# Gated linear attention prepared in 512-token parts beside the input projection, then run over 128-token pairs

## Time and profile before

| | us |
|---|---|
| median of 3 runs (2667.71 to 2677.51) | 2677.27 |
| profiled execution, its own time | 2677.31 |
| its span, first to last instruction | 2675.6 |

### The profile page before, as it was taken

The page is one execution under the profiler, slowest core; times in us unless marked ns, Lnnn a source line. Parts: engine busy times, 40 slices in busy tenths (PEclk is TensorE's granted clock), DMA queues, the critical chain, the costliest instruction groups (busy, mean ns, idle before and its releaser), DMA issues. The chain is left out here.

```text
span 2675.6 us, 34555 instructions
## 1 busy us (share of the span) xinstructions
PE 2281.3 (85%) x13572; PEld 1952.5 (73%) x13572; DVE 1440.0 (54%) x2273; ACT 954.2 (36%) x1399; POOL 360.6 (13%) x331
## 2 busy tenths in 40 slices
PE   7889999999247546629994799999999999999994
PEld 2368888888036346418883699999999999999993
DVE  3610016760576775276667555556555555555557
ACT  3611111111344232372220144444444444444444
POOL 1101000001320120020001101111111111111120
PEclk9899999999555565659996799999999999999997
DMA  7521101221222200534336256666656666665564
GB/s 268 190 59 68 65 24 64 73 102 47 63 54 72 62 8 17 212 128 164 115 114 231 94 204 221 220 220 220 212 203 202 215 218 202 208 215 203 204 215 192
DMA packets 161502, 392.50 MB, mean 147 GB/s; under 512 B 11988, under 2 KB 39412, under 8 KB 157332
## 3 DMA queue, kind: packets, MB, share of 16 engines
q1 hardware_dynamic: 136676, 299.89, 32.1%
q0 software_dynamic: 23600, 83.24, 9.9%
q10 hardware_dynamic: 1152, 8.39, 0.8%
HBM read 323.13 MB, written 68.35 MB: 146 GB/s over the span
## 5 line engine op out<-in xcount | busy, mean ns | idle before, releaser
L55 PE MATMUL bh<-xt_hi,shi 128*128 128x256 f32 x2048 | 580.5, 283 | 3.0 <-DVE slo L1859 3.0
L56 PE MATMUL bh<-xt_lo,shi 128*128 128x256 f32 x2048 | 580.4, 283 | 0.0
L57 PE MATMUL bh<-xt_hi,slo 128*128 128x256 f32 x2048 | 580.4, 283 | 0.0
L1859 DVE TENSOR_TENSOR slo<-raw,shi 128x1024 fp32r<-128x1024 f32 x384 | 455.6, 1222 | 155.4 <-ACT shi L1799 150.9
L1799 ACT ACTIVATE shi<-raw 128x1024 fp32r<-128x1024 f32 x384 | 388.9, 1050 | 130.6 <-PE eby L57 130.6
L55 PEld LDWEIGHTS bh<-xt_hi,shi 128*128 128x128 f32 x2048 | 394.1, 192 | 3.9 <-issue 3.4
L56 PEld LDWEIGHTS bh<-xt_lo,shi 128*128 128x128 f32 x2048 | 394.0, 192 | 0.6
L57 PEld LDWEIGHTS bh<-xt_hi,slo 128*128 128x128 f32 x2048 | 394.0, 192 | 0.0
L55 PE MATMUL bank<-h_hi,whi 128*128 128x512 f32 (+1 forms) x736 | 287.4, 391 | 7.3 <-DVE wlo L452 7.3
L56 PE MATMUL bank<-h_lo,whi 128*128 128x512 f32 (+1 forms) x736 | 287.2, 390 | 0.0
L57 PE MATMUL bank<-h_hi,wlo 128*128 128x512 f32 (+1 forms) x736 | 287.2, 390 | 0.0
(11 more groups left out here) (315 smaller groups left out, 3605.0 us busy)
## 6 DMA issues: line engine op xcount, KB each, us to landing
raw<-in_exp_w_dram SPq DMA_DIRECT2D x96, 2048.0 KB, 12.4
adaw<-in_ada_w_dram POOLq DMA_DIRECT2D x20, 1024.0 KB, 7.3
uT<-stage POOLq DMA_DIRECT2D x72, 256.0 KB, 2.3
wraw<-in_w_in_dram SPq DMA_DIRECT2D x22, 512.0 KB, 3.8
xb<-in_x_dram SPq DMA_DIRECT2D x16, 512.0 KB, 6.9
xt<-in_x_dram SPq DMA_DIRECT2D x16, 512.0 KB, 4.2
x2d<-xt SPq DMA_DIRECT2D x16, 512.0 KB, 2.6
h2d<-h SPq DMA_DIRECT2D x16, 512.0 KB, 2.9
```

The lines of the kernel that those rows point to most:

```text
L55: nc.tensor.matmul(out, w_hi, x_hi, start=start, stop=False)
L56: nc.tensor.matmul(out, w_hi, x_lo, start=False, stop=False)
L57: return nc.tensor.matmul(out, w_lo, x_hi, start=False, stop=stop)
L1859: nc.vector.tensor_tensor(item_dst(slo, n), item_src(n), item_dst(shi, n), ALU.subtract).then_inc(S["w_lo_ready"], 1)
```

## The change

It has three parts.

1. **Projection.** The tiles are in another order (decay inputs, keys, queries and values first, the gate last). TensorE's work is a list of slots, one unit each, in four banks; stage buffers are three, `wraw` is one. From slot 21 on, every third slot begins one of 20 parts: a head's 256 context tokens or 512 of its latent tokens. A part's work is dealt over the slots: logits and value transposes in its first (TensorE), Abs, Exp, Ln (ACT), scans (DVE); factors (ACT), keys (DVE), queries (POOL) in its second; transposes of the decayed keys ahead of the third slot's unit and four state updates (one per 128-token pair) behind it. The parts' inputs are loaded from `uT` by SP. Results go to DRAM: per head six arrays `prep` of 128 x 2048 (1 MB each), the transposed values, and `upd`, 18 pair updates. The decay bias is a 33rd row of the logits' product. The convolution works in two halves of 128 channels, its value taken from PSUM by DVE; the first half's taps are dealt over slots 52 to 74, the second's over slots 84 to 98.
2. **Heads.** The stage loads what was prepared. The state steps run over 128-token pairs: 16 in each direction and head, heads 0 and 1 first and interleaved, those of heads 2 and 3 behind the first four masks. The masks keep the whole 128 x 128 block, and two products of 64 x 64 per pair give the part of it between the two chunks. A state product has 128 columns.
3. **Last norm.** The squares of rows 0 to 7 move ahead in the last expert, the rows are scaled between the splits in smaller portions, and all groups but the first get their roots from ACT as Ln and Exp.

Core of the diff (lines that begin with # say where):

```diff
@@ phase_project @@
-    tiles = ([(OFF_A, "b")] + [(OFF_K + P * i, "b") for i in range(6)]
-             + [(256, "g"), (384, "g"), (0, "a"), (128, "a")]
-             + [(OFF_Q + P * i, "u") for i in range(2)] + [(OFF_R + P * i, "r") for i in range(4)]
-             + [(OFF_SC + P * i, "u") for i in range(6)])
+    V_OF = [OFF_V + P * h for h in range(HEADS)]
+    tiles = ([(OFF_A, "b"), (OFF_K, "b"), (OFF_Q, "u"), (V_OF[0], "b"), (V_OF[1], "b"), (OFF_K + P, "b"),
+              (OFF_Q + P, "u"), (V_OF[2], "b"), (V_OF[3], "b"), (256, "g"), (0, "a")]
+             + [(OFF_SC + P * i, "u") for i in range(6)] + [(384, "g"), (128, "a")]
+             + [(OFF_R + P * i, "r") for i in range(4)])
+    units = [(i, n) for i, (_, kind) in enumerate(tiles) for n in range(5 if kind == "b" else 4)]
+    NS = 3
+    START, PERIOD = 21, 3
+    parts = [(h, p) for h in range(HEADS) for p in range(5)]
+    begins = {START + PERIOD * j: j for j in range(NJ)}
+    NSLOT = max(NU + 1, START + PERIOD * NJ + 2)
 # SP, in its order per slot u: weights, part_loads(u+1), part_stores(u-2), update_store(u-4)
+                def part_loads(j):
...
+                    wait(sp, "logits_ready", j)
+                    sp.dma_start(af[0:32, 0:w], v.uT[OFF_A:OFF_A + 32, o:o + w]).then_inc(S["a_loaded"], 16)
+                    wait(sp, "v_turned", j)
+                    sp.dma_start(vt[:, 0:w], ...).then_inc(S["v_loaded"], 16)
+                    wait(sp, "k3x_ready", j)
+                    wait(sp, "k1_ready", lat_before(j))
...
+                        wait(sp, "q4x_ready", lat_before(j))
...
+                def part_stores(j):
...
+                    sp.wait_ge(S["v_read"], j + 1)
+                    sp.dma_start(v.vtok[h, :, 4 * (p - 1):4 * p, :], vtok[:, :, :]).then_inc(S["v_stored"], 16)
+                    sp.wait_ge(S["k3x_ready"], j + 1)
+                    sp.dma_start(v.prep[4, h, :, l], ke[:, :]).then_inc(S["k3x_stored"], 16)
...
 # GpSimd per slot u: store(u-1), middle(part begun at u), queries(part begun at u-1)
+                    pool.tensor_tensor(ch3(dm[:, :]), ch3(bs[:, :]), mg[:, 0, :].unsqueeze(2).to_broadcast(...), ALU.subtract
...
+                    pool.tensor_tensor(q1[:, :], q1[:, :], qd[:, :], ALU.mult).then_inc(S["q1_ready"], 1)
...
+                    pool.tensor_tensor(bs[:, :], bs[:, :], qd[:, :], ALU.mult).then_inc(S["q4x_ready"], 1)
...
+                    pool.tensor_tensor(ch3(q4[:, :]), ch3(bs[:, :]), fac_q[...], ALU.mult).then_inc(S["q4p_ready"], 1)
 # ACT
+                for u in range(NSLOT):
+                    if 0 < u <= NU:
+                        evict(u - 1)
+                    if u in begins:
+                        value_rows(begins[u])
+                        logs(begins[u])
+                    if u - 1 in begins:
+                        exps(begins[u - 1])
+                    if u - 2 in begins:
+                        key_rows(begins[u - 2])
+                    if u - 3 in begins:
+                        update(begins[u - 3])
+                    if u in first and first.index(u) + 1 < n_tiles:
+                        split(first.index(u) + 1)
 # DVE
+                start = [first[a_tiles[0]] + 5, first[a_tiles[1]] + 5]
+                stop = [first[g_tiles[1]], NU]
+                for u in range(NSLOT):
+                    if 0 < u <= NU and kind_of(u - 1) == "a":
+                        gated(u - 1)
+                    if u in begins:
+                        decays(begins[u])
+                    if u - 1 in begins:
+                        keys(begins[u - 1])
+                    if u in first and first.index(u) + 1 < n_tiles:
+                        split(first.index(u) + 1)
+                    for ch in range(2):
+                        if start[ch] <= u < stop[ch]:
...
+                                tap(ch, k)
 # TensorE
+                for u in range(NSLOT):
+                    if u in begins:
+                        j = begins[u]
+                        logits(j)
+                        pe.wait_ge(S["v_loaded"], 16 * (j + 1))
+                        wait(pe, "v_read", j)
+                        turn(vt, btv, j, "v_turned")
+                    if u - 2 in begins:
+                        j = begins[u - 2]
+                        pe.wait_ge(S["k3p_ready"], j + 1)
+                        wait(pe, "k_read", j)
+                        turn(kp, btk, j, "k_turned")
+                    if u < NU:
+                        unit(u)
+                    if u - 2 in begins:
+                        update(begins[u - 2])
@@ phase_gla @@
+        pre = [[sb(f"pre{n}{i}", [P, L]) for n in ("q1", "k1", "kc", "qx", "kx", "qp")] for i in range(2)]
+        vtok = [sb(f"vtok{i}", [P, PAIRS, P]) for i in range(2)]
+        state = [sb(f"state{g}", [P, PAIRS + 2, DV]) for g in range(HEADS)]
...
+                state_in(0)
+                state_in(1)
+                head_in(0)
+                state_in(2)
+                state_in(3)
+                head_in(1)
+                for g in range(HEADS):
+                    for n in range(NBAT):
+                        out(g * NBAT + n)
+                    if g + 2 < HEADS:
+                        head_in(g + 2)
 # scores(i): the 16 products of before, and per pair two of 64 x 64
+                            key, query = (0, CH) if early == 0 else (CH, 0)
+                            last = nc.tensor.matmul(score_banks[i % 2][early][half, j * P + query:j * P + query + CH],
+                                                    kx[half, o + key:o + key + CH], qx[half, o + query:o + query + CH],
+                                                    start=True, stop=True)
 # outputs(i): two products of 128 columns per pair
-                        for c in (0, 1):
...
+                        last = nc.tensor.matmul(bo[i % 2][:, j * P:(j + 1) * P], state[g][:, pair + 1, :],
+                                                pre[g % 2][5][:, pair * P:(pair + 1) * P], start=False, stop=True)
...
+                scores(0)
+                for i in range(len(BLOCKS)):
+                    if i + 1 < len(BLOCKS):
+                        scores(i + 1)
+                    outputs(i)
 # DVE
+                for k in range(NSTEP):
+                    for g in (0, 1):
+                        step(g, k)
...
+                for i in range(len(BLOCKS)):
+                    masks(i)
+                    if i < 4:
+                        for k in range(4 * i, 4 * i + 4):
+                            for g in (2, 3):
+                                step(g, k)
@@ phase_experts, ACT @@
+                        if last and f >= FD - 2:
+                            squares(*{FD - 2: (0, 2), FD - 1: (2, 4), FD: (4, 8)}[f])
+                    if last:
+                        nc.scalar.preload_act_table_set("natural_log_exp_and_others")
+                        root(4, 8)
+                        split(e, 18)
+                        squares(8, 10)
...
@@ phase_experts, DVE @@
+                        if last and f == FD - 1:
+                            roots(0, 4)
+                            normal(0, 1)
+                        if last and f == FD:
+                            normal(1, 4)
+                    if last:
+                        for i, (first, end) in enumerate([(4, 6), (6, 7), (7, 9), (9, 10), (10, 12), (12, 12)]):
+                            split(e, 18 + i)
+                            normal(first, end)
```

971 lines of the change are left out of this document (484 added, 487 removed).

## The result

The changed kernel takes 2572.51 us (median of 4 runs, 2567.61 to 2573.68) against 2677.39 us of the kernel before beside it (2667.71 to 2681.82): ratio 0.9608, 95% interval 0.9591 to 0.9625. The forecast was 2512, with a range to 2570. The direction was right and the time lies just above the range, so the working is what has to be explained: one term was too small by 95 us and another too small by 34 us on the other side.

The account below looks back on a forecast made before the run. TensorE was taken to bound the projection, a chain through all engines the heads stage, a DVE chain the tail. From 2677 us, +78 projection (54 + 6 + 15 + 3), -236 heads and -7 tail gave 2512; range 2448 to 2570.

Parts of the forecast that it names:

- Base of 523 us on TensorE, full price for what is inserted: Projection: TensorE alone sets the length, 99 units stay at 523 us, and anything inserted into its queue costs full price.
- +54 us of inserted work: Projection: TensorE's added logits, transposes and state updates, 2.98 us per 512-token part and about 1.5 per context part.
- +6 us where no taps run: Projection, parts 0 to 10 and the last: GpSimd shutting out DVE makes keys about 0.5 us late, 6 us in all.
- the 3 us given for all queues: Projection: allowance of 3 us for SP's loads and stores, GpSimd's stores and ACT's evictions queued behind waits.
- +15 us beside taps: Projection, slots 52 to 74: convolution taps between decays and keys delay six full parts by 2.5 us each.
- GpSimd and VectorE take turns: Projection: an exclusive lock adds GpSimd's 5 us per part to DVE's time; most of 21 us of stalls rests on it.
- Bound of +120: Projection: upper bound on the added time, with every full part 4 us late.
- the third rival: Projection: GpSimd, DVE and SP in one loop, late stores or taps cost each full part 4 us; 2554 us, chance 0.11.
- Heads -236 us: Heads stage: first outputs end at S + 44, then 15 blocks of 9 us at half clock; gain 236 us.
- the first rival: Heads stage: full clock, blocks 4.9 instead of 9 us, 49 less, 2463 us; against it, half clock at 930 to 940; chance 0.22.
- second rival: Heads stage: loads bound it, prepared tensors moving at 256 instead of 420 GB/s, 35 us more, 2547 us; chance 0.11.
- Tail -7: Last norm: fewer chains of small DVE operations at the end, net 7 us gained, bounds 2 and 10.

Follow-up runs that it names:

- the kernel with order and taps: Changed kernel with SyncE's list in order of readiness and no taps between a part's decays and keys: projection 630.3 us, kernel 2490.81 us, ratio 0.931.
- f3: Changed kernel with SyncE's list in readiness order, later weight loads, moved taps, quarter loads, dealt state steps, second buffers for sums and value rows: 2462.4 us, ratio 0.9189.
- k3: Changed kernel with f3's projection, whole-head loads, ScalarE issuing output stores, head g+1's steps dealt over head g's blocks: heads stage 152.5 us, kernel 2457.93 us, ratio 0.9182.

## Why the prediction was wrong, step by step

- *Base of 523 us on TensorE, full price for what is inserted.* Right: with the ring opened, the projection takes 603.2 us, 538.0 + 65.2, of which 57.0 are more busy time of TensorE and the rest is waits.
- *+54 us of inserted work.* The step was right and so nearly was the sum: 57.0 us of busy time at clock 0.99. By records, which overlap their neighbours, it is 66.6 us in the kernel with order and taps (clock 0.97), and two terms were too small. Eight transposes are 25.4 / 18 = 1.41 us a part and not the 0.88 that halving gave, logits 1.21 and not 1.04; the updates, 1.08, were right. Halving a half-clock price assumes that nothing but columns is paid for.
- *+6 us where no taps run.* Measured 30.2. The chain from logits to keys was well priced; its start was not. This is the step that failed: the sentence "Slack 1.5 us, eaten only if a store of 256 KB lands late" together with the 3 us given for all queues. I took 2.3 us for a landing, that of single stores on another queue; seven in a row on one queue land after medians of 3.8 to 7.3 us, and I had listed the values' copy behind its store, but not the scan behind the sums' store, nor SyncE behind the weight split. Each is a small wait; they close a ring, so each part hands its lateness to the next.
- *+15 us beside taps.* Measured 47.9. The place was right: with the taps moved 7.9 of them are left. But part of it was the ring's: SyncE's order alone brought them to 35.3, and moving the taps took 18.6 us from the stage, with SyncE's order repaired 31.1.
- *Half clock after a stall.* Not in the prediction at all: some 29 us of longer busy time.
- *GpSimd and VectorE take turns.* Seen (0.68 us becomes 1.77), and of little weight on this path: one of four products less bought 3.0 us, and with all four in place f3 has 8.0 us of waits for keys left. What I put 21 us on, in the main as that lock's doing, was mostly the ring's.
- *Bound of +120.* It was every part 4 us late; the stage has 57 us of inserted work, 78.0 + 7.5 of waits and some 29 of lost clock, +173 with 1 us of rest. It is the third rival's mechanism (late stores, taps, one loop), at more than twice its price.
- *Heads -236 us.* Measured -270.4. First outputs were copied at S + 40.5 (S + 44 forecast); the states came at 426 GB/s, not 256 (the loads of the earlier trace rows at 690 to 700 were for the most part keys and queries, 64 rows in each transfer, and not loads like the states'). Then 15 blocks took 106 us, 7.1 each, not 9: the first rival's full clock held in part, and the stops before heads 2 and 3 (5.0 and 3.9 us of waits) threw it back each time. The argument against it, the stretch at 930, was of 64-column products, and that difference, which I had written down as "for it", decided, be it by the width or by the number of weight loads that goes with it: with 64 columns the clock stays at half and the stage is 84 us longer.
- *Loads as a bound* (second rival): not for 8 KB rows, except for the 36.5 us at the start, which the state steps cover in part. With rows of 2 KB DMA was busy 0.95 of f3's stage; rows of 4 KB in place of 8 took 21 us from k3's.
- *Tail -7.* Measured -8.2, and -8.1 alone. Right.

In sum 78 - 236 - 7 = -165 was forecast and 172.9 - 270.4 - 8.2 = -105.7 came.

## What to carry to other kernels

When one engine issues all loads and stores of a software pipeline, write its list in the order in which things become ready, follow every buffer around the ring (who must have stored it, whose wait stands ahead of that store in the list), and price a store by rows with as many transfers queued behind each other as the new kernel has. Adding time between rounds doesn't open a ring that the issue order closes; reordering alone gave 50 us here; order, weights, taps and two buffers together gave 108. An edit that lengthens the list (28 loads for 7) moves everything behind it: what the next engine waits for first has to stand ahead. A stall on TensorE is to be charged with the half clock behind it, and a full-clock forecast needs rows with products of the same shape.

## What the hardware showed that I had not expected

- The granted clock was 0.50 through 190 us of unbroken fp32 products whose outputs had 64 columns, and rose to 1.00 with the same data in 128-column outputs. At half clock the records of both come at the same pitch, 0.21 us.
- Loads by length of row: 8 KB rows moved 426 GB/s, 4 KB rows 370 to 402, and 2 KB rows 304 on average with DMA 0.95 busy (output stores included). The states' loads in 9 KB rows are among those at 426 GB/s here. The loads of the earlier trace rows that moved 256 had rows of 8 and 9 KB, but four of the five large ones filled only 64 partitions each; whether that is the reason was not tried.
- Of seven 256 KB stores issued in a row on one queue, the first lands in a median of 3.8 us and the last two in 7.3 and 7.2; a single one on another queue lands in 2.3. Whether this is the queue alone or also the loads beside it was not tried.
